# The second block of an expert's tokens is cut from 128 rows to 64, and its two float parts share one stationary tile

## The reference

```
logits = h @ w_router + b_router                  # 1024 x 32
top_logits, top_idx = top_k(logits, 4)            # 4 experts for each token
gu  = x_e @ w_gate_up[e] + b_gate_up[e]           # rows x 2048
act = min(gate, 7) * sigmoid(1.702 * gate) * (clip(up, -7, 7) + 1)
y   = act @ w_down[e] + b_down[e]                 # rows x 1024
out[token] += g2 * top_weight * y
```

```
138 106  19 367  62 153 158 154 117 110  46  63 149 130 145 120
130 236 115  86  46  36 164 165 101 157  92 105  91 192 112 231
```

## Time and profile before

| | us |
|---|---|
| runs, median (range) | 2564.94 (2564.0 to 2570.42) |
| profiled execution, its own time | 2563.14 |
| its span, first to last instruction | 2561.5 |
| TensorE matmul busy | 2382.6 (93%) |
| TensorE weight load busy | 1929.0 (75%) |
| VectorE busy | 1710.3 (67%) |
| ScalarE busy | 1204.2 (47%) |
| GpSimd busy | 688.0 (27%) |
| mean granted TensorE clock | 0.969 of full |

### The profile page before, as it was taken

How to read it: one execution, slowest core, us unless ns; L and a number is a source line. 1 busy time by engine, 2 the same in 40 slices (tenths; PEclk the granted TensorE clock), 3 DMA queues, 4 the chain that set the end, 5 groups by cost and what they waited for, 6 DMA issues and landing times.

```text
span 2561.5 us, 37686 instructions
## 1 busy us (share of the span) xinstructions
PE 2382.6 (93%) x11145; PEld 1929.0 (75%) x11146; DVE 1710.3 (67%) x2187; ACT 1204.2 (47%) x1591; POOL 688.0 (27%) x733
## 2 busy tenths in 40 slices
PE   6899994887919999999999999999999999999997
PEld 2678873765817888888888888888888888888885
DVE  2683425664755787856589865586699667689674
ACT  2332103663224655644467544454477445466462
POOL 1252105970241231311122310131034112133120
PEclk9899997998958999999999999999999999999998
DMA  7233107842317796956589965595599767699680
GB/s 236 74 115 132 54 1 211 231 136 107 137 40 265 265 324 207 369 199 200 187 297 368 327 196 181 188 312 192 178 377 359 256 190 257 226 308 370 196 297 15
DMA packets 280931, 549.39 MB, mean 214 GB/s; under 512 B 23265, under 2 KB 52977, under 8 KB 278769
## 3 DMA queue, kind: packets, MB, share of 16 engines
q1 hardware_dynamic: 250192, 463.93, 52.8%
q0 software_dynamic: 27328, 72.24, 10.2%
q10 hardware_dynamic: 3362, 12.59, 1.3%
HBM read 510.22 MB, written 47.38 MB: 218 GB/s over the span
## 4 chain that ended last, share of the span: by engine, by line
PE 65%; DVE 3%; issue 2%; DMA 1%; POOL 0%; DVEq 0%; ACT 0%; POOLq 0%; ACTq 0%
PE psum L1843 59%; PE psum L1831 3%; PE psum L1801 2%; PE psum L1792 2%; DVE d_wlo L1696 1%; DVE d_act L1714 0%; DVE d_up L1708 0%; DMA d_raw<-in_w_gate_up_dram 0%; DMA d_xg<-xn_d,d_entry 0%; DVE d_glu L1702 0%; DVE d_atlo L1719 0%; POOL d_dest L1562 0%; ACT d_sg L1638 0%; POOL d_raw L1572 0%; POOL out_dram L1540 0%
## 5 line engine op out<-in xcount | busy, mean ns | idle before, releaser
L1626 ACT ACTIVATE d_whi<-d_raw 128x1024 fp32r<-128x1024 f32 x530 | 540.9, 1060 | 307.5 <-PE psum L1843 284.9
L1696 DVE TENSOR_TENSOR d_wlo<-d_raw,d_whi 128x1024 fp32r<-128x1024 f32 x530 | 625.4, 1220 | 72.2 <-ACT d_whi L1626 72.2
L1843 PE MATMUL psum<-d_whi,d_xthi 128*128 128x512 f32 x1536 | 611.6, 398 | 0.8 <-DVE d_xtlo L1687 0.8
L1843 PE MATMUL psum<-d_whi,d_xtlo 128*128 128x512 f32 x1536 | 606.8, 395 | 0.0
L1843 PE MATMUL psum<-d_wlo,d_xthi 128*128 128x512 f32 x1536 | 606.8, 395 | 0.0
L1540 POOL DMA_INDIRECT out_dram<-d_yst,d_dest x49 | 80.2, 1636 | 1082.8 <-DVE d_yst L1729 1077.1
L1843 PEld LDWEIGHTS psum<-d_whi,d_xthi 128*128 128x128 f32 x1536 | 289.8, 189 | 68.1 <-issue 2.7
L1843 PEld LDWEIGHTS psum<-d_whi,d_xtlo 128*128 128x128 f32 x1536 | 289.8, 189 | 68.1
L1843 PEld LDWEIGHTS psum<-d_wlo,d_xthi 128*128 128x128 f32 x1536 | 290.3, 189 | 65.8
L1696 DVE TENSOR_TENSOR d_wlo<-slab,d_whi 128x1024 fp32r<-128x1024 f32 x268 | 317.0, 1220 | 26.7 <-ACT d_whi L1626 20.9
L1626 ACT ACTIVATE d_whi<-slab 128x1024 fp32r<-128x1024 f32 x268 | 273.5, 1058 | 95.2 <-PE psum L1843 83.5
(11 more groups left out here) (281 smaller groups left out, 3320.8 us busy)
## 6 DMA issues: line engine op xcount, KB each, us to landing
slab<-in_w_gate_up_dram SPq DMA_DIRECT2D x132, 1024.0 KB
d_raw<-in_w_gate_up_dram SPq DMA_DIRECT2D x132, 1024.0 KB, 8.7
d_raw<-in_w_down_dram SPq DMA_DIRECT2D x132, 1024.0 KB, 7.0
b_wp<-in_w_ada_dram POOLq DMA_DIRECT2D x16, 1024.0 KB, 8.1
slab<-in_w_in_dram SPq DMA_DIRECT2D x12, 1024.0 KB, 5.6
slab<-in_w_ada_dram SPq DMA_DIRECT2D x8, 1024.0 KB, 5.1
b_q<-q_d SPq DMA_DIRECT2D x24, 256.0 KB, 8.9
b_k<-k_d SPq DMA_DIRECT2D x24, 256.0 KB, 9.3
```

Source lines behind the costliest of these rows:

```text
L1626: nc.scalar.activation(whi[n % NW][:, part, :], raw[n % NRAW][:, part, :], ACT.Copy).then_inc(whi_ok, 1)
L1696: nc.vector.tensor_tensor(wlo[n % NW][:, part, :], raw[n % NRAW][:, part, :], whi[n % NW][:, part, :].bitcast(F32), ALU.subtract).then_inc ...
L1843: mm = nc.tensor.matmul(to, m_[b][:, KH * h + k, :], w_[n % NW][:, k, :], start=(h == 0 and k == 0 and q == 0), stop=(h == 1 and k == KH - ...
```

## The change

The second block of a group now holds at most 64 tokens. Its high and low parts lie side by side in one 128-column stationary tile (`xt2`, `at2`: columns 0 to 63 high, 64 to 127 low), and each weight tile takes two products instead of three: [hi lo] x high weights and [hi lo] x low weights. PSUM rows 0 to 63 then hold the high part's results, rows 64 to 127 the low part's. The two row halves are added on the way out: ScalarE copies the lower rows to SBUF, VectorE adds the upper rows to them, and the rest works on the sum. (The product of the two low parts is in the sum now.) A group steps by 128 tokens, not by 256; the last group of an expert has a second block where 1 to 64 tokens are left over. So an expert with up to 128 tokens has one group of one block, with 129 to 192 one group of two, with 193 to 256 two groups of one block, and so on. The table's second row holds, for each expert, the group from which two blocks are taken. The table is computed with fewer VectorE instructions, its constants are set ahead of the mixer's steps, and its scratch lies in `s.modacc`.

```
 # mixer: table
+                nc.vector.memset(s.table[:, :, :], 0)
+                nc.vector.memset(cnt[:, 4 * E:5 * E], 1.0)
+                for g in range(T // P):
+                    nc.vector.memset(thr[:, g, :], float(g * P + P // 2) if g else -1.0)
                 steps(dve, step)
...
-                for g in range(1, T // s.GB):
-                    own.link(nc.vector.tensor_scalar(more, n, float(g * s.GB), None, ALU.is_gt))
-                    own.link(nc.vector.tensor_tensor(groups, groups, more, ALU.add))
+                own.link(nc.vector.tensor_tensor(
+                    more[:, :, :], thr[:, :, :], n.rearrange("p (a e) -> p a e", a=1).broadcast_to([1, T // P, E]),
+                    ALU.is_lt))
+                own.link(nc.vector.tensor_reduce(groups, more[:, :, :].rearrange("p g e -> p e g"), AX_X, ALU.add))
                 own.link(nc.vector.tensor_tensor_scan(ends, ones_e, groups, 0.0, ALU.mult, ALU.add))
-                own.link(nc.vector.memset(s.table[:, :, :], 0))
+                own.link(nc.vector.scalar_tensor_tensor(two, groups, float(P), n, ALU.mult, ALU.is_lt))
...
 # loop
-                        with eng.If((g - gs) * GB + P < n):
+                        with eng.If(g + 1 > two_at):
...
 # GpSimd, set-up of the expert stage
+                own.link(nc.gpsimd.memset(xg[1][HB:, :], 0.0))
+                own.link(nc.gpsimd.memset(act_t[1][HB:, :], 0.0))
...
 # ScalarE
+                def xt_two(count):
+                    act.wait_ge(xt_mm[1], 2 * count)
+                    nc.scalar.activation(xt2[:, :, 0:HB], turned_x[:, :, 0:HB], ACT.Copy).then_inc(xthi_ok[1], 2)
+                def low_rows(to, j):
+                    return nc.scalar.activation(to, psum[HB:P, 2 * (j % 3) + 1, :], ACT.Copy)
+                def gate_rows(g, i):
+                    act.wait_ge(gu_mm, 2 * GU * g + 2 * (2 * i) + 2)
+                    low_rows(gate_two[:, :], 2 * i).then_inc(gate_low, 1)
+                def y_rows(g, jd):
+                    act.wait_ge(dn_mm, DN_CRED + 2 * DN * g + 2 * jd + 2)
+                    low_rows(y_two[jd][:, :], GU + jd).then_inc(y_low, 1)
...
                     if blocks == 2:
-                        xt(1, g + 1)
+                        xt_two(g + 1)
                     else:
                         act.sem_inc(xthi_ok[1], 2)
+                        for copied in (gate_low, up_low):
+                            act.sem_inc(copied, 2)
...
                         if n in (2, 6):
-                            for b in range(blocks):
-                                sigmoid(g, n // 4, b, sh)
+                            sigmoid(g, n // 4, 0, sh)
+                            if blocks == 2:
+                                gate_rows(g, n // 4)
+                                sigmoid(g, n // 4, 1, sh)
+                        if n in (4, 8) and blocks == 2:
+                            up_rows(g, n // 4 - 1)
...
+                        if n == 11:
+                            if blocks == 2:
+                                y_rows(g, 0)
+                            else:
+                                act.sem_inc(y_low, 2)
...
+                    if blocks == 2:
+                        y_rows(g, 1)
 # VectorE
+                def both_halves(rows, j):
+                    return nc.vector.tensor_tensor(rows, psum[0:HB, 2 * (j % 3) + 1, :], rows, ALU.add)
+                def gate_rows(g, i):
+                    dve.wait_ge(gate_low, 2 * g + i + 1)
+                    both_halves(gate_two[:, :], 2 * i).then_inc(gate_sum, 1)
...
                 def clipped(g, i, b, sh):
...
+                        dve.wait_ge(up_low, 2 * g + i + 1)
+                        both_halves(up_two[:, :], 2 * i + 1).then_inc(up_sum, 1)
+                        dve.wait_ge(up_sum, 2 * g + i + 1)
+                        value = up_two[:, :]
...
                 def output(g, jd, b, sh):
...
+                        dve.wait_ge(y_low, 2 * g + jd + 1)
+                        both_halves(y_two[jd][:, :], GU + jd).then_inc(y_sum, 1)
+                        dve.wait_ge(y_sum, 2 * g + jd + 1)
+                        value = y_two[jd][:, :]
...
                     else:
                         dve.sem_inc(xt_ok[1], 2)
+                        for done in (gate_sum, up_sum, y_sum):
+                            dve.sem_inc(done, 2)
 # TensorE, half()
-                        mm = nc.tensor.matmul(to, pick[:, :], bhl[:, at:at + SL], start=False, stop=last)
+                        mm = nc.tensor.matmul(to[0:ROWS[b], :], pick[:, 0:ROWS[b]], bhl[:, at:at + SL], start=False, stop=last)
...
-                    hi, lo = (xthi, xtlo) if j < GU else (athi, atlo)
+                    if b == 0:
+                        hi, lo = (xthi, xtlo) if j < GU else (athi, atlo)
+                        products = ((hi, whi), (hi, wlo), (lo, whi))
+                    else:
+                        hilo = xt2 if j < GU else at2
+                        products = ((hilo, whi), (hilo, wlo))
```

More of the change, by code:

```diff
@@ L958, in mixer_block @@
         slot = [[sb(f"c_slot{i}_{r}", [P, 1], I32) for r in range(K4)] for i in range(2)]
-        cnt = sb("c_cnt", [1, 6 * E], F32)
+        counting = s.modacc[0:1, 2 * D:2 * D + 21 * E]
+        cnt = counting[:, 0:5 * E]
+        thr, more = (counting[:, (5 + 8 * k) * E:(13 + 8 * k) * E].rearrange("p (g e) -> p g e", e=E)
+                     for k in range(2))
         w_in, small_in, slab_in = sem("c_w_in"), sem("c_small_in"), sem("c_slab_in")
@@ L1257, in _ @@
                 dve.wait_ge(cnt_mm, 1)
-                n, more, groups, ends, ones_e = (cnt[:, k * E:(k + 1) * E] for k in range(5))
+                n, groups, ends, two, ones_e = (cnt[:, k * E:(k + 1) * E] for k in range(5))
                 own.link(nc.vector.tensor_copy(n, psum[0:1, 7, 0:E]))
-                own.link(nc.vector.memset(groups, 1.0))
-                own.link(nc.vector.memset(ones_e, 1.0))
-                for g in range(1, T // s.GB):
-                    own.link(nc.vector.tensor_scalar(more, n, float(g * s.GB), None, ALU.is_gt))
-                    own.link(nc.vector.tensor_tensor(groups, groups, more, ALU.add))
+                own.link(nc.vector.tensor_tensor(
+                    more[:, :, :], thr[:, :, :], n.rearrange("p (a e) -> p a e", a=1).broadcast_to([1, T // P, E]),
+                    ALU.is_lt))
+                own.link(nc.vector.tensor_reduce(groups, more[:, :, :].rearrange("p g e -> p e g"), AX_X, ALU.add))
                 own.link(nc.vector.tensor_tensor_scan(ends, ones_e, groups, 0.0, ALU.mult, ALU.add))
-                own.link(nc.vector.memset(s.table[:, :, :], 0))
+                own.link(nc.vector.scalar_tensor_tensor(two, groups, float(P), n, ALU.mult, ALU.is_lt))
                 own.link(nc.vector.tensor_copy(s.table[:, 0, 1:E + 1], ends))
-                own.link(nc.vector.tensor_copy(s.table[:, 1, 0:E], n))
+                own.link(nc.vector.tensor_tensor(s.table[:, 1, 0:E], ends, two, ALU.subtract))
             @block.tensor
@@ L1583, in body @@
                     for b in range(2):
-                        fetch(b, e, gs, g)
+                        fetch(b, e, gs, g, b < blocks)
                     stored(g)
@@ L1841, in half @@
                             pe.wait_ge(wlo_ok, RAW_CRED + 2 * NH * g + 2 * n + k // 2 + 1)
-                        for q, (m_, w_) in enumerate(((hi, whi), (hi, wlo), (lo, whi))):
-                            mm = nc.tensor.matmul(to, m_[b][:, KH * h + k, :], w_[n % NW][:, k, :],
+                        for q, (m_, w_) in enumerate(products):
+                            mm = nc.tensor.matmul(to, m_[:, KH * h + k, :], w_[n % NW][:, k, :],
                                                   start=(h == 0 and k == 0 and q == 0),
-                                                  stop=(h == 1 and k == KH - 1 and q == 2 and j > 0))
+                                                  stop=(h == 1 and k == KH - 1 and q == len(products) - 1 and not closes))
                         if b == blocks - 1 and k % 2 == 1 and counted(n, k // 2):
                             mm.then_inc(w_free, 1)
-                    if h == 1 and j == 0:
-                        if b == 0:
-                            pe.wait_ge(pick_ok, g + 1)
+                    if closes:
+                        pe.wait_ge(pick_ok, g + 1)
                         mm = bias(True)
```

142 lines of the change are left out of this document (87 added, 55 removed).

## The result

| | before | after |
|---|---|---|
| median (range) of four runs, us | 2565.7 (2564.0 to 2570.42) | 2448.11 (2447.04 to 2450.74) |
| profiled execution, its own time | 2563.14 | 2447.04 |
| its span | 2561.5 | 2445.4 |

The ratio is 0.954, 95% interval 0.9524 to 0.9557: faster. The forecast was 2463, range 2437 to 2499. For an execution like the profiled one it said 2461.6; 2447.0 came, 14.6 less. The mechanism was right. Four terms of the sum were too large, by 22 together, and two too small, by 8.

The account below looks back on a forecast made before the run. TensorE was taken to bound the kernel, with VectorE binding too in one-block groups that load tables. Terms from -132.0 for fewer products to +13.7 summed to -101.5 from 2563.1, giving 2463 us after a median adjustment, range 2437 to 2499.

Parts of the forecast that it names:

- parts 1, 2: Expert stage: new group counts, and two products for three in each second block, together -132.0 us.
- part 3: Second block's 64-column bias tile: 144 changes of stationary width at 0.095 us each, +13.7 us, ends 0 and 52.
- part 4: Two-block groups: ScalarE copies and VectorE adds joining the row halves stay hidden behind TensorE, 0, above 12 us.
- part 5: End of a two-block group: VectorE waits for the last y's sum, 1.45 us before seven one-block groups, +10.2 us.
- rival C: Hand-overs between ScalarE and VectorE stop TensorE and its clock falls: slower than before, 2593 us; 4 in 100.
- part 6: One-block groups: three more VectorE semaphore increments behind `pick`, 0.1 us each, +6.0 us, from -1 to 12.
- parts 7, 8: GpSimd's two set-up memsets on the chain, +1.6 us; ten small VectorE memsets ahead of the mixer's steps, +0.5 us.
- The first group: Start of the expert stage: 7.3 us left over for waiting and the lower clock, taken to stay.
- part 9: Last group, now of one block: one scatter instead of two, -1.5 us, from -2 to 0.
- part 10: Weight loads for 36 groups instead of 33: the DMA queue keeps pace, 0; 12 us if it does not.
- Rival B: Width changes cost nothing and VectorE's delays are absorbed: 2439 us; 17 in 100.
- D: Groups not as counted, two-block ones rarer; with none, some 10 us over before; 1 in 100.

Follow-up runs that it names:

- e6: Changed kernel with a third product (high weights again) for each weight tile of the second block: 2580.11 us.
- e1: Changed kernel with the second block's bias matmul over all 128 columns and rows, so no width change is left: 2448.36 us.
- e2: Changed kernel with TensorE taking the second block first in the last half tile of a two-block group: 2436.53 us.
- e7: Changed kernel with VectorE making the add of a two-block group's last y once more, into a spare tile: 2444.94 us.
- e3: Changed kernel with VectorE's three increments for the missing block moved from `pick` to behind the fifth weight tile: 2441.95 us, one execution.
- e10: Changed kernel with the second clip and activation one weight tile earlier in one-block groups: 2454.41 us.
- e13: Changed kernel with two edits, second block first in the last half tile and increments behind the fifth weight tile: median 2430.91 us, ratio 0.9472 to before.
- e14: Changed kernel with only the increments moved behind the fifth weight tile, five rounds: median 2442.91 us, ratio 0.9503 to before.
- e4: Changed kernel with two expert-stage set-up memsets moved from GpSimd to VectorE: 2449.25 us.
- e15: The kernel before, unedited, run once more for a second look at its first group, which took 79.6 us.
- e9: Changed kernel with the table's threshold moved so that every block is a group of its own: 2580.44 us.

## Why the prediction was right, and where its sizes were off

By its own steps, for the profiled execution (-101.5 forecast, -116.1 measured):

- **Groups and products (parts 1, 2, -132.0): right.** D' is 61.3, the counts are 12, 20 and 4, and e6 takes the gain back. (48 x 0.23 is 11.0, not the 11.1 that part 2 writes; a matmul takes 0.231, so 11.1 is what came.)
- **Width changes (part 3, +13.7): 0.** The step that failed is the carrying over of 0.095 from the earlier trace rows, where 1-column tiles give way and the row count changes too. The 64-column tile has the ordinary distance, and e1 shows no difference. The Trainium skill, TensorEngine Tiling (Array Packing), "Tiling Modes", says that a change of tiling mode drains TensorE. These 144 changes of width don't, so either they are no change of mode or they need no drain; the runs don't tell which.
- **Hand-overs in a D' (part 4, 0): right.** PE has no idle time in any D' but the first group's 0.06.
- **The last y (part 5, +10.2): right in mechanism, short in size.** `pick` went from 3.77 to 5.16, 1.4 for the forecast 1.45, and S behind a D' to 38.8 as forecast; e2 and e7 show the cause from both sides. But the forecast stopped at the wait and left out the clock, which it had priced for rival C: three falls, +4.6. What decides whether a group falls is open: falls are absent in e2, e3, e10, e13 and e14, whose waits are shorter, but in e6 too, whose wait is the same.
- **Increments (part 6, +6.0): +3.8.** 0.1 each is right (e3), but 0.1 came back from the earlier `pick`. Part 6 had named a shorter comparison for its lower end; that this is it is not shown. The 13 S not behind a D' are 0.13 over the 37.0 of the sum, not 0.3: 13 x 0.17 = 2.2 less.
- **Memsets and mixer (parts 7, 8, +2.1): +4.8.** Each was priced by its own length; what they pushed GpSimd's next instructions into was not looked at (e4). Of the 4.8, 4.7 lie behind `d_yst`'s memset. That this memset itself comes only 0.1 later than before (748.52 for 748.42) is luck, since it moves by 10 from run to run; part 8 is therefore neither confirmed nor refuted.
- **The first group (left as it was): -5.4.** 61.3 and the 7.3 make 68.6, and 63.2 came: a residual was booked as fixed that the change removed (e15). What part of the change shortens the weights' time under way is open; it is not the products (e6) nor the memsets (e4 has 5.2 as well), and the smaller gather fits but is not tested.
- **Tail (part 9, -1.5): -2.6.** One scatter at the end for two.
- **DMA (part 10, 0): right** (e9).

Sum of the differences: -13.7 + 4.9 (the falls, and 7 x 0.05) - 2.2 + 2.7 - 5.4 - 1.1 = -14.8, for -14.6. The total flatters the terms: 7.6 too little hides a third of the 22.4 too much. Rival B, 2439, had the first half of its condition right (changes cost nothing) and the second wrong (VectorE's delay is not absorbed in an S); C and D had nothing to show.

## What to carry to other kernels

Where two engines bound a stage within about 1% of each other (36.6 and 37.0 here), price every microsecond put in front of the less busy one's queue as lost, at the place where the other asks for the result, however much later; then look whether the order of the other engine's own work can take it back, as two changes of order did here for 15 us. A saving in an engine's work is read off the distance of its instructions, not off their listed lengths, and a residual of the profile (a long first group) is looked into before it is booked as fixed.

Times of single runs are best compared by stages: a start that moves by 10 us hides an effect of 4, and the same effect is plain from a mark at the stage's own beginning.

## What the runs showed of the hardware

- Stationary tiles of 128 and 64 columns can alternate at 0.23 us a matmul of 512 columns; 64 output rows fewer change nothing either.
- A semaphore increment that VectorE issues by itself took 0.1 us: three of them made the distance to the next split 0.51 instead of 0.22.
- A cast of 32 elements for each partition took GpSimd 0.21 us in one place and 4.48 in another, where it ended at 759.19, 0.07 after a burst of four VectorE splits (754.50 and 4.62), as if it had stood still for all four; a copy of one element for each partition 3.12 beside a VectorE split of 3.35, and 0.18 elsewhere. The 4.48 stood in the changed kernel and nine of the runs behind it alike, and was 5.19 in e7. The Trainium skill, SBUF — State Buffer, "SBUF: two separate sides", has a rule for this: a VectorE instruction with two SBUF inputs and a GpSimd one that reads SBUF block each other for a whole instruction. The trace agrees, and the cast's end just behind the burst suggests that the wait went on over four of them in a row.
- Behind waits of 1.8 us of TensorE (2.2 from start to start) the granted clock fell in 3, 2, 3, 2 and 0 of 7 cases in five kernels with the same schedule there; behind waits of 1.5 to 1.6 us in none of 21. Waits of 2.23 and 2.27 from start to start also passed without a fall. Each fall cost 1.5 to 1.6 us.
